# A hybrid encoder block on one core: the conditioning sums of the last chunk, taken beside the output projection

## The reference

```python
mod = c_act @ w_ada[l] + b_ada[l]
sh1, sc1, g1, sh2, sc2, g2 = [t[:, None, :] for t in jnp.split(mod, 6, axis=-1)]
h = rms_norm(x, norm1_gain[l]) * (1.0 + sc1) + sh1
x = x + g1 * token_mixer(h, w_in[l], conv_w[l], q_gain[l], k_gain[l], sink[l], w_o[l])
h = rms_norm(x, norm2_gain[l]) * (1.0 + sc2) + sh2
x = x + g2 * conv_ffn(h, w_up[l], ffn_conv_w[l], ffn_conv_b[l], w_down[l])
```

## Time and profile before

| | us |
|---|---|
| three runs | 805.96, 807.36, 808.68 (median 807.36) |
| the profiled execution, its own time | 808.3 |
| its span | 806.2 |
| TensorE busy (matmuls) | 774.8 (96%) |
| VectorE busy | 515.6 (64%) |
| ScalarE busy, GpSimd busy | 374.2 (46%) each |
| DMA moved | 96.03 MB |

### The profile page before, as it was taken

The page is one execution under the profiler, slowest core; times in us unless marked ns, Lnnn a source line. Parts: engine busy times, 40 slices in busy tenths (PEclk is TensorE's granted clock), DMA queues, the critical chain, the costliest instruction groups (busy, mean ns, idle before and its releaser), DMA issues.

```text
span 806.2 us, 10380 instructions
## 1 busy us (share of the span) xinstructions
PE 774.8 (96%) x3709; PEld 644.4 (80%) x3709; DVE 515.6 (64%) x722; ACT 374.2 (46%) x664; POOL 374.2 (46%) x223
## 2 busy tenths in 40 slices
PE   3889999999999999999999999999999999999997
PEld 3677787788888888878889988888888888888886
DVE  5847876658765976686638799888888988000000
ACT  7665467455654575556524454434443343112220
POOL 2774423343453345244863255554444555444340
PEclk9999999999999999999999999999999999999999
DMA  8943342243414341533143042223333322323311
GB/s 301 381 146 116 134 155 78 72 164 131 158 54 181 131 157 52 184 130 108 57 150 105 4 154 85 75 100 104 104 104 104 98 75 76 104 92 118 131 52 40
DMA packets 83279, 96.03 MB, mean 119 GB/s; under 512 B 2674, under 2 KB 77610, under 8 KB 83242
## 3 DMA queue, kind: packets, MB, share of 16 engines
q1 hardware_dynamic: 79018, 93.44, 34.0%
q10 hardware_dynamic: 4224, 2.10, 0.8%
HBM read 93.43 MB, written 2.10 MB: 118 GB/s over the span
## 4 chain that ended last, share of the span: by engine, by line
PE 85%; DVE 9%; ACT 3%; issue 2%; DMA 1%; SPq 0%; DVEq 0%
PE bank L832 25%; PE bank L833 25%; PE bank L834 25%; PE bank L964 2%; PE bank L992 2%; PE bank L975 2%; DVE acc L1283 1%; DVE bank L1195 1%; DVE pt_lo L1347 1%; DMA ada<-in_w_ada_dram 1%; DVE a_buf L1371 1%; DVE sm L1333 1%; DVE prob L1326 1%; PE bank L881 1%; PE bank L880 1%
## 5 line engine op out<-in xcount | busy, mean ns | idle before, releaser
L832 PE MATMUL bank<-h_hi,w_hi 128*128 128x512 f32 (+1 forms) x760 | 294.8, 388 | 2.3 <-DVE q_st L1245 2.3
L833 PE MATMUL bank<-h_lo,w_hi 128*128 128x512 f32 (+1 forms) x760 | 292.4, 385 | 0.0
L834 PE MATMUL bank<-h_hi,w_lo 128*128 128x512 f32 (+1 forms) x760 | 292.2, 384 | 0.0
L450 POOL TENSOR_TENSOR w_lo<-w_raw,w_hi 128x1024 fp32r<-128x1024 f32 x76 | 194.8, 2585 | 195.4 <-ACT w_hi L546 188.1
L457 POOL TENSOR_TENSOR w_lo<-w_raw,w_hi 128x512 fp32r<-128x512 f32 x88 | 123.8, 1428 | 181.1 <-ACT w_hi L546 181.1
L546 ACT ACTIVATE w_hi<-w_raw 128x1024 fp32r<-128x1024 f32 x120 | 122.5, 1052 | 100.4 <-PE bank L834 100.4
L832 PEld LDWEIGHTS bank<-h_hi,w_hi 128*128 128x128 f32 x760 | 143.4, 189 | 30.0 <-issue 2.7
L834 PEld LDWEIGHTS bank<-h_hi,w_lo 128*128 128x128 f32 x760 | 143.6, 189 | 28.7
L833 PEld LDWEIGHTS bank<-h_lo,w_hi 128*128 128x128 f32 x760 | 143.7, 189 | 26.5
L832 PE MATMUL bank<-g_hi,w_hi 128*128 128x512 f32 x176 | 69.2, 393 | 0.0
L834 PE MATMUL bank<-g_hi,w_lo 128*128 128x512 f32 x176 | 68.6, 390 | 0.0
(11 more groups left out here) (186 smaller groups left out, 1056.9 us busy)
## 6 DMA issues: line engine op xcount, KB each, us to landing
w_raw<-in_w_in_dram SPq DMA_DIRECT2D x23, 1024.0 KB, 5.1
w_raw<-in_w_up_dram SPq DMA_DIRECT2D x21, 1024.0 KB, 4.9
ada<-in_w_ada_dram SPq DMA_DIRECT2D x32, 512.0 KB, 6.0
ada<-in_w_ada_dram SPq DMA_DIRECT2D x32, 256.0 KB, 6.3
w_raw<-in_w_down_dram SPq DMA_DIRECT2D x8, 1024.0 KB, 4.7
w_raw<-in_w_o_dram SPq DMA_DIRECT2D x4, 1024.0 KB, 4.9
w_raw<-in_w_down_dram SPq DMA_DIRECT2D x4, 768.0 KB, 4.2
x_nat<-in_x_dram SPq DMA_DIRECT2D x4, 512.0 KB, 5.2
```

The source lines that it names most:

```text
L450: pool.tensor_tensor(lo_of(n, u), raw(n)[:, :, u * P:(u + 1) * P], hi_of(n, u), SUB).then_inc(lo_ready, 1)
L832: pe.matmul(dst, w_h, rhs_hi, start=first, stop=False)
L833: pe.matmul(dst, w_h, rhs_lo, start=False, stop=False)
L834: return pe.matmul(dst, w_l, rhs_hi, start=False, stop=last)
```

## The change

The eight multiply-adds of chunk 3 leave pass 3. Two of them come ahead of the residuals of the output projection, the others after residuals 1 to 5. SyncE issues pieces 0 and 1 as before, pieces 2 to 5 after the load of `P_WO + 2`, pieces 6 and 7 after that of `P_WO + 3`, all ahead of the load of `third_raw`. TensorE's two turns come after the second half of the first up pair, into banks 7 and 6, and VectorE's reduces after the last tile of h2, ahead of the up loop. Passes 0 to 2 keep their order.

```diff
-        GEMV_AT = {n + 1: n for n in range(KT)}
+        EVEN = {2 * n + 4: n for n in range(KT)}
+        GEMV_AT = [EVEN, EVEN, EVEN, {}]
...
                     load(None, 0, pair_of(g, i), wi[:, :, col:col + PC])
-                    if i >= 3:
+                    if i >= 3 and 2 * i - 6 < (2 if g == KV - 1 else KT):
                         ada_load(g, 2 * i - 6)
                         ada_load(g, 2 * i - 5)
...
                 load(None, 0, P_WO + n, wo[:, :, n * PC:(n + 1) * PC])
-                if n < 2:
-                    ada_load(KV - 1, 4 + 2 * n)
-                    ada_load(KV - 1, 5 + 2 * n)
+                for k in {2: range(2, 6), 3: range(6, KT)}.get(n, ()):
+                    ada_load(KV - 1, k)
...
             for n in range(1, D // PC - 1):
-                ada_turn(KV - 1, n - 1)
                 pair(None, 0, P_WO + n, WO_BANK[2 * n:2 * n + 2], wo_parts)
-            pe.wait_ge(m_free, ada_use(KV - 1, 1) + 1)
+
+            def gate_turn():
+
+                pe.wait_ge(ada_done, KV * (KT - 1))
+                for a in range(2):
+                    for f in range(HT):
+                        mm = pe.transpose(bank[MB - a][:, f * P:(f + 1) * P],
+                                          acc[:, (a * HT + f) * P:(a * HT + f + 1) * P], ident[:, :])
+                    mm.then_inc(mod_done, 1)
...
                 up_half(P_UP, 2, 1, k)
+            gate_turn()
             for k in range(KT):
                 up_half(P_UP + 1, 4, 1, k)
...
+                src = bank[MB - a if c == KV - 1 else MB]
                 dve.tensor_reduce(st[:, 7, a * HT:(a + 1) * HT],
-                                  bank[MB][:, :].rearrange("p (f n) -> p f n", n=P), AX.X, ADD).then_inc(m_free, 1)
+                                  src[:, :].rearrange("p (f n) -> p f n", n=P), AX.X, ADD).then_inc(m_free, 1)
...
-                    if kind and slot // 2 - 1 in GEMV_AT:
-                        gemv(g, GEMV_AT[slot // 2 - 1])
+                    if slot in GEMV_AT[g]:
+                        gemv(g, GEMV_AT[g][slot])
...
+            for k in range(2):
+                gemv(KV - 1, k)
             for f in range(KT - 1):
...
-                if f in (1, 3):
-                    ada_sums(KV - 1, f // 2)
...
                     square_add(dve, g_, sum_done, y_buf, b_buf, ADD)
+                for k in {1: (2, 3), 2: (4,), 3: (5,), 4: (6,), 5: (7,)}.get(f, ()):
+                    gemv(KV - 1, k)
...
             h2_low(2 * KT - 1)
+            for a in range(2):
+                ada_sums(KV - 1, a)
```

## The result

The changed kernel took 814.59 us in the median (four runs, 813.97 to 816.09), the kernel before 808.02 beside it (805.96 to 809.43). The ratio is 1.0069, 95% interval 1.0045 to 1.0093: slower, which is the sign that was forecast (forecast 811.5), but the median lies 1.1 us above the upper end of the range. Measured once more, beside the last of the experiments, the ratio was 1.0049 (1.0030 to 1.0068).

A forecast was written before the change was run, and what follows sets the result against it. TensorE's busy time was taken to bound the kernel; -1.78 + 3.3 + 0.88 + 1.7 + 0 = +4.1 us gave a profiled 812.4 and a median of 811.5. Range 805.2 to 813.5.

The forecast's parts named there:

- The last pass, -1.78: Last pass: TensorE's wait for a transposed probability tile's low half vanishes, winning 1.78 us (1.0 to 1.78).
- third_raw at 419.9 to 420.5: Output projection: the first up-projection tile, queued behind the last conditioning load, lands at 419.9 to 420.5, 5.6 us too late.
- The delay of the turn, 3.3: End of output projection: late low parts and port turns delay TensorE's turn of the sums by 3.3 us (1.0 to 4.5).
- The transposes, +0.88: Between the up projection's halves: eight transposes extend a stretch without TensorE waits, +0.88 us; leaving the projection wins nothing.
- The clock, +1.7: After the wait at the turn of the sums: TensorE's granted clock dips, costing 1.7 us (0 to 2.9).
- rival D: Dip covers turn to spread (2.9) and first low parts miss TensorE in the up loop (0.5): +5.8, 813.2; chance 0.07.
- rival C: Turn of the sums late but the clock stays up: +2.4 us, 809.8; chance 0.17.
- The up loop, 0: Ahead of the up loop: VectorE's first convolution starts about 1.3 us late, slack absorbs it: 0, at worst 0.5.
- the likeliest case's own range: Whole kernel: the forecast case alone was given 810.3 to 813 us; its chance was 0.42.
- A: Output projection: the cover holds, the half sum is there when TensorE comes; 805.6 us, chance 0.16.
- B: Multiply-add 7 keeps the ports one turn more, half sum only 1.0 late, no dip: +0.1, 807.5; chance 0.13.
- E: Last pass: VectorE is late by another wait and the 1.78 stays; 813.3 us, chance 0.05.

The follow-up runs named there:

- v2: Kernel before with slot 8 of the last pass left empty, multiply-adds 2 to 7 of chunk 3 one even slot later; ratio 0.9981, repeated 0.9976.
- the later load alone: Kernel before with the first up pair's load held until GpSimd made the first low unit of the last output pair; ratio 1.0013.
- the fill: Changed kernel with 18 unread 512-column matmuls ahead of the turn of the half sums, keeping TensorE busy; ratio 1.0030 to the kernel before.
- the first experiment: Changed kernel with the load of the first up pair ahead of conditioning pieces 6 and 7; ratio 1.0036 to the kernel before.

## Why the prediction was right or wrong

**The last pass, -1.78: right, with less to spare than was thought.** -1.77, and -1.72 to -1.77 in every other kernel without the multiply-add at 350.86. One of the eight carried all of it, as v2 shows. The working had the first low half done at 354.3, 0.8 ahead of TensorE. That is when it begins (355.45 in the changed kernel, where all times up to here read 1.11 later), and the matmul that needs it starts 0.74 after that, as before (356.09 and 356.83):

```profile
355.45 1.28 DVE L1356 TENSOR_TENSOR pt_lo<-bank,pt_hi 128x512 fp32r<-128x512 f32 x2
...
355.94 0.39 PE L834 MATMUL bank<-h_hi,w_lo 128*128 128x512 f32 x1
356.19 0.50 PE L992 MATMUL bank<-pt_hi,v_st 128*128 128x512 f32 x1
```

TensorE could have started it at 356.17. So there was no slack of 0.8, and that nothing of the 1.78 was lost is partly luck.

**third_raw at 419.9 to 420.5: right, by two sizes that offset each other.** On the clock of before (0.66 added to the traced times from here to the turn) the last conditioning load went out at 413.45, ahead of the forecast 413.7 to 414.3, and the pair of loads took 7.1 us to land instead of 6.2, so that ScalarE could begin at 420.5. The high parts and GpSimd's start at 421.7 (forecast 421.0 to 421.5) followed.

**The delay of the turn, 3.3: right, and its rule shown.** +3.30, in the second trace +2.96. That it is 3.30 to the hundredth is luck: GpSimd started 0.2 behind the forecast times, and VectorE's turns took 1.9 us of its 11.75 and not 2.35. The sum at 429.44 of the kernel before didn't end with GpSimd's operation at 430.2, as the working reads it, but 0.28 later, at 430.48. In eleven of the twelve traces besides that of before (the changed kernel's two and ten of the experiments) the second half sum ends about 0.3 after the end of GpSimd's last low part, whatever moved that end; the twelfth is the later load alone, where it ends 0.3 behind the operation before. The Trainium skill, "SBUF — State Buffer", section Who interferes with whom, states that the pair of ports which the two engines share is locked for a whole instruction. All thirteen traces agree with it in this sum. How the 3.3 come about isn't a sum of two parts: with the load early and the multiply-adds in place +1.6, with the load late and multiply-add 7 gone +2.4, with a later load and no multiply-adds +0.8. What decides in these traces is when GpSimd ends and which of its two 2.4 us operations the second half sum falls behind, and both causes push on that.

**The transposes, +0.88: right** (+0.86). Alone they give back 0.5 in the projection; in the changed kernel that is lost in the wait, as said.

**The clock, +1.7: the step that failed.** That the clock would fall after the wait was right; the size of the term was not. The 1.7 was what a single dip of the start of the run lacked in granted clock. The one in the changed kernel was twice as long and lay on the chain from the turn to the spread:

```profile
428.00:442.00 14.00, 8.32 (x45) 7.83 (x44) 8.65 (x21) 3.06 (x8) 5.31 (x3) 0.76 0.44 150
```

A mean of 0.76 over 14 us lacks 3.4 us. It cost 2.45 on the way to the spread and 0.23 behind it, 2.7 together, near the 2.9 that stood as the term's far end and was given to rival D only; the fill took 2.7 back. In the second trace the same stretch has 0.88, which lacks 1.7, and the cost was 1.3. So a dip of the forecast size occurs too, and why one execution has twice the length of the other is open. The comparison of idles by their length, with which rival C was argued down (none after 1.8 us, one after 2), doesn't hold either: 3.0 us in the first experiment were followed by none.

**The up loop, 0: right in sum, wrong in its size on VectorE.** The addition behind the two reduces fell behind a GpSimd operation and took 2.42 us for eight elements a partition, so the first convolution came some 3.3 late and not 1.3. Of that, GpSimd's next low parts took over only 1.0 (7.55 us after the first matmul of the loop, against 6.59). TensorE didn't wait: 346.04 to the end against 346.02.

**The range.** The sum of the stages, +5.1 in place of +4.1, lies within the likeliest case's own range (810.3 to 813, which is +2.9 to +5.6). The median is 3.1 above the forecast: 1.0 by the clock's term, 0.7 since the median of before was taken from three runs as exact (it moved from 807.36 to 808.02 with a fourth), and 1.4 that no stage of the table holds. Nothing had been allowed for where the start of a run ends up; that the 1.4 lie there is likely but not shown. In the second measurement the medians are 4.1 apart (812.63 and 808.52). A range of absolute times must hold that scatter beside the mechanism's. Of the rivals, A and B fell by the wait, C by the dip, E by the pass; what happened is the forecast with the first half of D.

## What to carry to other kernels

Before moving a block of work out of a busy stretch, find the single instruction of it that is late for somebody: here one of eight, and one empty slot gave the whole gain. When a transfer that waits for work is put into a queue, everything behind it in that queue inherits the wait; look for the one that another chain needs, and at which operations of the other engine sharing its ports it will then meet. Cost an idle of TensorE on a chain as its length plus up to what half clock adds to the work right behind it, and give that addition a range from 0: here it was 0, 1.3, 1.5 and 2.7 us.

## What the runs showed of the hardware

- VectorE and GpSimd took turns, also where VectorE had its next operation ready: multiply-add 7 stood right behind a square sum and still waited out a GpSimd operation (2.31 us for 1.28). In this pattern a short operation on the critical chain costs up to about one GpSimd operation of 2.4 us (a half sum of 0.42 alone took 2.33 with multiply-add 7 left out). Even tiny ones wait: 1.28 us for two elements, 2.42 for eight:

```profile
461.70 2.42 DVE L1279 TENSOR_TENSOR mod<-st,par 128x8 f32<-128x8 f32 x1
```

- The length of an idle didn't tell whether TensorE's clock would dip. Ahead of the turn of the sums, after 3.0 us (the first experiment) it stayed at 1.00, after 3.8 the next 4.8 us had 0.64 in the mean, after 4.4 and 4.7 us the way to h2 lost 1.3 and 2.7 us. In the start of the run 2.2 us were enough, and that each time: all thirteen profiles have a wait at this place, in five it is 2.0 us by the profile and the mean clock of 95 to 110 us is 0.89, in eight it is 0.9 and the clock 1.00. In the kernel before and in the changed one (the wait, then the stretch):

```profile
97.29 1.11 PE L964 MATMUL bank<-k_st,q_st 128*128 128x384 f32 x4 [2.00 <-DVE prob L1326]
95.00:110.00 15.00, 13.00 (x55) 10.30 (x54) 11.25 (x17) 7.41 (x17) 5.23 (x4) 0.89 0.41 141
...
100.01 1.11 PE L964 MATMUL bank<-k_st,q_st 128*128 128x384 f32 x4 [0.86 <-DVE prob L1335]
95.00:110.00 15.00, 14.14 (x68) 11.33 (x67) 14.12 (x24) 8.94 (x21) 6.13 (x4) 1.00 0.53 175
```

  Earlier idleness doesn't explain it: in the kernel before TensorE was busy for all of the 18.40 us from 76.50 to 94.90. What decides between these cases was not tested.
